# Stick-breaking scores from stacked rounded halves, stacked softmax queries, another opening order, spectra stored by another queue

## The chip, the cores and the metric
The kernel runs as one program on one core of one Trainium2 chip. The metric is the device time of one execution in microseconds (us). The kernel before takes 2325.8 us (median of three runs, 2324.95 to 2327.99). Its engines are called PE (TensorE, the matrix engine), DVE (VectorE), ACT (ScalarE), POOL (GpSimd) and SP (SyncE, which here only issues transfers).

## The reference, cut to what matters
Two blocks of two layers each, batch 1, 512 tokens, width 1024. The four places that the change touches:

```
# opening: S5 mixer
h = rms_norm(x, norm_mix[0]);  u = h @ w_in                    # (512, 1024)
ab, bb, c  ->  y = scan(u) ...                                  # complex recurrence over 64 groups

# stick-breaking attention, 16 heads of 64
z = einsum('bhqd,bhkd->bhqk', q * 64**-0.5, k)                  # float32, causal blocks only
log_one_minus = where(causal, log_sigmoid(z) - z, 0)
rem = reverse_cumsum(log_one_minus) - log_one_minus
w = where(causal, exp(log_sigmoid(z) + rem), 0);  o = w @ v

# softmax attention, first 8 of 16 heads: 8 query heads, 2 key heads, 512 queries x 768 keys
q_a, k_a = rope(rms_norm(q_a)), rope(rms_norm(k_a))             # rope on the 512 latent tokens only
s = q_a . k_a * 64**-0.5;  p = softmax(s);  o = p @ v_a

# hyena mixer: spectra of 4 filters of 512 channels, scaled and used later
k_f = rfft(filters);  z = irfft(rfft(z) * k_f) ...
```

## The kernel before, in words
All work is one straight program for each engine, written by hand; engines wait for each other on semaphores that only count up. Activations lie with channels in the partitions (8 tiles of 128 channels x 512 tokens). PSUM has 8 banks of 512 float32 columns; `take` reserves one and waits until its last reader has released it, `fills` and `frees` signal full and free.

Matrix products have two forms. In plain float32 one `matmul` of the program becomes two records of the trace. In the split form each operand is a rounded part (type fp32r, written by ACT) and a rest (value minus rounded part, written by DVE or POOL), and a product is three fp32r matmuls: hi x hi, hi x lo, lo x hi. The big layers use the split form (`lin_split`); the weight halves are rounded by ACT (`split_hi`) and their rests taken by POOL (`split_lo`, L1458).

*Opening.* SP issues its transfers in program order: parameters, `cols`, the four quarters of x, the constants `mats`, then the first weight panel, the B and C parameters, three more panels. PE first sums the squares of x for the norm (`norm("mix0")`, L417), then computes u = x W (L475) as eight tiles (nb, jt) of 6.9 us; the norm's scale is applied when ACT copies a tile out (L1137), which needs `R4` (DVE L1698). DVE and POOL build the tables of the recurrence beside it.

*Stick-breaking attention* (PE L679 to L725). `scores(h)` makes four causal blocks of 512, 384, 256 and 128 columns in plain float32: `KZ[:, h]` holds the 64 rows of head h and zeros in the other 64, so the full 128 rows of `Q` can be streamed. After each block a bfloat16 product of two constant matrices adds the mask (L681). ACT makes softplus of the scores (`Abs` L1233, `Exp` L1235, `Ln` in two parts L1240), DVE adds and splits it (L1913, L1915, L1917), PE adds running sums (`cumulate`, L691, L697, L710), and ACT's `weights` (L1247) takes the exponential, which also releases the banks of head h. PE's order is scores(h), cumulate(h-1), and for odd h the value products of two heads (`values`, L725). scores(h+1) uses the banks of head h-1, so it waits for `weights(h-1)`.

*Softmax attention.* After norms and rope, 64 turns n (head, query tile): `sm_scores(n)` on PE (two products of 384 keys, L840 for n < 32, L842 after), `sm_max` on DVE (L1974, L1978), `sm_exp` on ACT (L1303), six transposes (`sm_turn(n-2)`, L852), copied out half by ACT (L1086) and half by DVE (L1994), value products for two turns (`sm_values`, L874, L878), and a gate every fourth turn (DVE L2003, L2005). Before it DVE rotates four query tiles and one key tile (L1946, L1947, L1951), the eight products `qm` (L799) and others run on PE meanwhile.

*Spectra.* For each of four filter groups u: PE makes filters (L927), DVE decays and adds them (L2069, L2085), ACT and POOL sum absolute values (L1340, L1539), PE reduces them (L919) and transforms (L945), DVE combines (L2108 to L2111) into one buffer `SPO`, and POOL stores that to memory twice for each group (`spectra_out`, L1525). The hyena input layer (split form, 32 halves) follows.

Of the kernel before, what the change touches and what calls it, by code (L numbers as in the profile page):

```python
# [27 lines left out]
P = 128  # L28
# [42 lines left out]
def build(nc, A, out):  # L71
    ctx = ExitStack()
    with ctx:
# [38 lines left out]
        def col(n, i=0, r=P):  # L112
# [12 lines left out]
            "conv_base", "silu_ready", "kz_zero", "ln_ready", "sp_raw", "cum_done", "s_lat",  # L125
            "rn_ready",
            "w3_in",
# [50 lines left out]
        slots_used = [SLOTS]  # L178
# [127 lines left out]
        KZ = bigv(0, 8192).rearrange("p (h t) -> p h t", h=HEADS)  # L306
        VT = bigv(8192, 4096).rearrange("p (s n) -> p s n", s=4)
        Q = bigv(12288, 4096).rearrange("p (k t) -> p k t", k=KT)
# [14 lines left out]
        KZ2 = bigv(4096, 2 * LA).rearrange("p (h t) -> p h t", h=2)  # L323
        PR = [bigv(5632 + LA * i, LA) for i in range(3)]
# [79 lines left out]
        def _(pe):  # L404
# [57 lines left out]
            pe.wait_ge(S["consts_in"], 16)  # L462
            norm("mix0")

            for nb in range(4):
                s, wp = panel(pe, A["ssm_w_in"][nb][:, :], KT)
                for jt in range(2):
                    key = ("u", nb, jt)
                    o = take(pe, key, bank=(2 + 2 * nb + jt) % 4)
                    for jj in range(2):  # L470
                        for k in range(KT):
                            if nb == 0 and jt == 0 and jj == 0:
                                h_wait(k)
                            t0 = (2 * jt + jj) * P
                            i = pe.matmul(o[:, jj * 256:jj * 256 + 256], H[:, k, t0:t0 + P], wp[:, k, :],  # L475
                                          start=k == 0, stop=k == KT - 1)
                    fills(i, key)
                    if nb == 0 and jt == 0:
                        o = take(pe, ("rb", "mix0"), bank=1)
# [190 lines left out]
            def scores(h):  # L670
                key = ("z", h)
                o = take(pe, key, bank=3 * (h % 2), n=3)
                if h == 0:
                    pe.wait_ge(S["masks_ready"], 2)
                    for t in range(8):
                        pe.wait_ge(*free(("k", t)))
                        pe.wait_ge(*free(("q", t)))
# [107 lines left out]
            panel_done(s, full(key))  # L785
            lin("gate", A["in_gate"], 4, lat, beside=lambda m: norm(SMALL_NORMS[4 + m]) if m < 5 else None)
# [37 lines left out]
            def sm_scores(n):  # L824
# [3 lines left out]
                if n == 0:  # L828
                    pe.wait_ge(S["roped"], 7)
                if n == 32:  # L830
                    pe.wait_ge(S["roped"], 15)
# [118 lines left out]
            enter_halves([full(("f", 1, 1, 3))])  # L950
            lin_split(lambda t: (f"z{t // 8}" if t < 24 else "zg", t % 8), A["hy_in"], 32, h_hi_wait("nw1"), h_lo_wait("nw1"),
# [68 lines left out]
        def _(sp):  # L1020
# [4 lines left out]
            for i in range(4):  # L1025
                put(X[:, 2 * i:2 * i + 2, :], A["x"][:, 2 * i:2 * i + 2, :], f"x_in{i}")
            put(mats[:, :], A["mats"][:, :], "consts_in")
            for n, (src, dst, landed, after) in enumerate(loads):
                if n == 1:
                    put(BRAW[:, :, :, :], A["ssm_b"][:, :, :, :], "bc_in")  # L1030
                    put(CC[:, :, :, :], A["ssm_c"][:, :, :, :], "bc_in")
                for w in after:
# [9 lines left out]
        def _(act):  # L1042
# [75 lines left out]
            act.wait_ge(S["cols_in"], 16)  # L1118
            act.activation(small[:, 616:632], cols[:, COLS["c"]:COLS["c"] + 16], ACT.Silu).then_inc(S["s_lat"], 1)
            act.preload_act_table_set("sqrt_and_others")  # L1120
            for k in range(4, KT):
# [5 lines left out]
                  ("norm", "mix0"))  # L1127

# [83 lines left out]
            for t in range(8):  # L1212
# [3 lines left out]
                act.wait_ge(S["kz_zero"], t // 2 + 1)  # L1216
                act.wait_ge(*full(key))
                step(act.activation(KZ[0:64, 2 * t, :], ps(key)[0:64, :], ACT.Copy))
                own()
                frees(act.activation(KZ[64:128, 2 * t + 1, :], ps(key)[64:128, :], ACT.Copy), key)  # L1220
            for q in range(8):
                split_hi(HALVES_AT["v"] + q + 2)
            for t in range(8):
                split_hi(HALVES_AT["q"] + t + 2)
                evac(("q", t), Q[:, t, :], scale=HD ** -0.5)

            def softplus(h):
# [176 lines left out]
        def _(pool):  # L1404
# [76 lines left out]
            for m in range(8):  # L1481
                pool.wait_ge(*full(("down0", m)))
            for i in range(4):
                pool.memset(KZ[:, 4 * i:4 * i + 4, :], 0.0).then_inc(S["kz_zero"], 1)
                split_lo(HALVES_AT["k"] + 2 + i)
            for n in range(HALVES_AT["k"] + 6, HALVES_AT["ffn1"]):
# [13 lines left out]
            for t in range(8):  # L1500
                pool.wait_ge(*full(("gate", t)))
            pool.memset(bigv(4096, 2 * LA), 0.0).then_inc(S["kz_zero"], 1)
# [6 lines left out]
            pool.wait_ge(S["roped"], 15)  # L1509
# [10 lines left out]

            def spectra_out(u):
                for f in range(2):
                    n = 2 * u + f
                    pool.wait_ge(S["spec_used"], n + 1)
                    pool.dma_start(spec[u // 2, u % 2, f], SPO[:, :]).then_inc(S["spec_out"], 16)  # L1525

            for u in range(4):
# [15 lines left out]
                if u:  # L1543
                    spectra_out(u - 1)
            spectra_out(3)
# [11 lines left out]
        def _(dve):  # L1557
# [102 lines left out]
            dve.wait_ge(*free(("norm", "mix0")))  # L1660
            dve.reciprocal(rows_of("mix0"), rows_of("mix0")).then_inc(S["rn_ready"], 1)

# [34 lines left out]
            dve.wait_ge(*full(("rb", "mix0")))  # L1697
            frees(dve.tensor_copy(R4, ps(("rb", "mix0"))[:, 0:P:32]), ("rb", "mix0"))  # L1698
# [7 lines left out]
            own()  # L1706
            step(TS(BB[:, 1, :, :], BB[:, 1, :, :], -1.0, None, ALU.mult))
# [189 lines left out]
            norm_split("mix1", lambda k: col("mix1", k), r=rms[:, 0:L])  # L1897
            for c in range(2):
                for t in range(4):
                    key = ("v", c, t)  # L1900
                    dve.wait_ge(*full(key))
                    frees(dve.tensor_copy(VT[:, t, c * 512:c * 512 + 512], ps(key)), key)
            dve.tensor_copy(NEGTRI, mat("negtri")).then_inc(S["neg_ready"], 1)
# [36 lines left out]
            dve.wait_ge(S["kz_zero"], 5)  # L1940
            for t in range(5):
# [8 lines left out]
                if t < 4:  # L1950
                    TT(q, q, rt, ALU.add).then_inc(S["roped"], 1)  # L1951
                else:
                    for hh in range(2):
                        rr = slice(64 * hh, 64 * hh + 64)
                        TT(KZ2[rr, hh, LC:LA], q[rr, :], rt[rr, :], ALU.add).then_inc(S["roped"], 1)
                        step(dve.tensor_copy(KZ2[rr, hh, 0:LC], KA2[rr, 0:LC]))
            own()
            dve.sem_inc(S["roped"], 1)
# [424 lines left out]
```

## Time and profile before
| | us |
|---|---|
| runs | 2324.95, 2325.8, 2327.99; median 2325.8 |
| profiled execution | 2322.11, of it 2320.3 in the span of the engines |
| PE busy | 2176.5 (94%) |
| DVE busy | 1263.3 (54%) |
| ACT busy | 736.0 (32%) |
| POOL busy | 685.1 (30%) |
| mean granted PE clock | 0.966 of full speed |

PE is busy for 94% of the span, and a busy share says nothing of what it is busy with: a plain float32 product and a slow clock both count as busy. Where PE sits idle, the profile names what it waited for. Times are counted from the start of the span.

### The profile page before, as it was taken

The page shows a single profiled execution, that of the slowest core. Times are in us where ns is not written, and L with a number is a line of the kernel's source. Part 1 is how long each engine was busy: PE and PEld are TensorE (multiplying, and loading weights), DVE is VectorE, ACT ScalarE, POOL GpSimd, SP SyncE. Part 2 cuts the span into 40 slices and gives each one's busy share as a digit, 9 for nine tenths or more (in the row PEclk, how much of TensorE's full clock was granted, in tenths as well). Part 3 has the DMA queues.
Part 4 walks back from the last instruction along what each step waited for, and adds up shares of the span by engine and source line. Part 5 has one row for each costly group of instructions (what it writes and reads, how often), then busy time and mean ns, then how long its engine had stood idle before and what let it go on. Part 6 is the DMA issues. An engine that isn't in the chain of part 4 may idle for free. (4 is left out here: it accounts for less than half of the span.)

```text
span 2320.3 us, 27423 instructions
## 1 busy us (share of the span) xinstructions
PE 2176.5 (94%) x10821; PEld 1581.0 (68%) x10821; DVE 1263.3 (54%) x2299; ACT 736.0 (32%) x1035; POOL 685.1 (30%) x405
## 2 busy tenths in 40 slices
PE   7959899999999988999999999999999989999988
PEld 6847688888868766688888855436774436885653
DVE  8562389984352166378872032357773574235861
ACT  3423332231242365332322131325441332332110
POOL 6513344445444300345444400010000342441000
PEclk9979899999989999999999989989999979999999
DMA  4033244434423200244433231110002113322101
GB/s 177 2 49 93 73 141 149 140 122 127 138 73 91 82 1 1 82 136 136 146 125 100 75 120 55 59 36 21 1 1 73 73 73 118 100 91 91 73 19 73
DMA packets 50576, 193.66 MB, mean 83 GB/s; under 512 B 9225, under 2 KB 9401, under 8 KB 45231
## 3 DMA queue, kind: packets, MB, share of 16 engines
q1 hardware_dynamic: 36288, 140.14, 19.3%
q0 software_dynamic: 10432, 50.59, 6.0%
q10 hardware_dynamic: 3728, 1.18, 0.3%
q8 instruction: 86, 1.41, 0.2%
q14 instruction: 42, 0.34, 0.0%
HBM read 179.04 MB, written 10.49 MB: 82 GB/s over the span
## 5 line engine op out<-in xcount | busy, mean ns | idle before, releaser
L1458 POOL TENSOR_TENSOR w_lo<-raw,w_hi 128x1024 fp32r<-128x1024 f32 (+1 forms) x216 | 513.5, 2378 | 834.3 <-ACT w_hi L1096 834.1
L583 PE MATMUL psum<-h_hi,w_hi 128*128 128x512 f32 x1216 | 485.8, 400 | 10.1 <-ACT h_hi L1103 8.5
L584 PE MATMUL psum<-h_hi,w_lo 128*128 128x512 f32 x1216 | 478.2, 393 | 0.0
L1096 ACT ACTIVATE w_hi<-raw 128x1024 fp32r<-128x1024 f32 (+1 forms) x216 | 224.9, 1042 | 611.1 <-PE psum L588 400.6
L588 PE MATMUL psum<-h_lo,w_hi 128*128 128x512 f32 x1216 | 302.1, 391 | 0.0
L583 PEld LDWEIGHTS psum<-h_hi,w_hi 128*128 128x128 f32 x1216 | 230.4, 189 | 72.8 <-ACT h_hi L1103 15.9
L584 PEld LDWEIGHTS psum<-h_hi,w_lo 128*128 128x128 f32 x1216 | 231.1, 190 | 45.8 <-issue 0.2
L588 PEld LDWEIGHTS psum<-h_lo,w_hi 128*128 128x128 f32 x1216 | 229.4, 189 | 47.9
L452 PE MATMUL psum<-big,ring 128*128 128x512 f32 x480 | 208.7, 593 | 0.0
L452 PEld LDWEIGHTS psum<-big,ring 128*128 128x128 f32 x480 | 90.7, 190 | 113.7 <-issue 112.9
L630 PE MATMUL psum<-f_hi,w_hi 128*128 128x512 f32 x352 | 137.6, 391 | 0.0
L631 PE MATMUL psum<-f_hi,w_lo 128*128 128x512 f32 x352 | 137.1, 389 | 0.0
L632 PE MATMUL psum<-f_lo,w_hi 128*128 128x512 f32 x352 | 137.0, 389 | 0.0
L1086 ACT ACTIVATE big<-psum 128x384 f32<-128x384 f32 (+5 forms) x142 | 72.8, 538 | 178.9 <-PE psum L852 79.7
L1766 DVE TENSOR_TENSOR X<-psum,X 128x512 f32<-128x512 f32 x24 | 16.6, 691 | 184.6 <-PE psum L632 147.1
L1786 DVE SCALAR_TENSOR_TENSOR sq<-sq,small 128x128 f32<-128x128 f32 x210 | 104.0, 544 | 2.5
L1786 DVE SCALAR_TENSOR_TENSOR sq<-ffn_buf,small,sq 128x128 f32<-128x128 f32 x210 | 101.8, 534 | 2.5
L1198 ACT ACTIVATE ffn_buf<-psum,cols 128x512 f32<-128x512 f32 x44 | 34.4, 781 | 197.3 <-PE psum L588 197.3
L630 PEld LDWEIGHTS psum<-f_hi,w_hi 128*128 128x128 f32 x352 | 66.1, 188 | 14.3
L632 PEld LDWEIGHTS psum<-f_lo,w_hi 128*128 128x128 f32 x352 | 66.1, 188 | 13.8
L631 PEld LDWEIGHTS psum<-f_hi,w_lo 128*128 128x128 f32 x352 | 66.1, 188 | 13.2
L1576 DVE RECIPROCAL rms<-rms 128x512 f32<-128x512 f32 (+1 forms) x9 | 27.0, 2997 | 83.0 <-ACT rms L1075 83.0
(365 smaller groups left out, 3327.2 us busy)
## 6 DMA issues: line engine op xcount, KB each, us to landing
raw<-in_ffn_w_up SPq DMA_DIRECT2D x88, 512.0 KB, 3.7
raw<-in_ffn_w_down SPq DMA_DIRECT2D x32, 512.0 KB, 3.6
raw<-in_hy_in SPq DMA_DIRECT2D x32, 512.0 KB, 3.5
ffn_buf<-in_ada_w POOLq DMA_DIRECT2D x20, 512.0 KB, 5.0
sq<-in_ada_w POOLq DMA_DIRECT2D x20, 512.0 KB, 5.0
raw<-in_ssm_w_glu SPq DMA_DIRECT2D x16, 512.0 KB, 3.6
spec<-big POOLq DMA_DIRECT2D x8, 1024.0 KB, 4.1
big<-spec POOLq DMA_DIRECT2D x8, 1024.0 KB, 5.1
```

The costliest lines, as they stand in the source:

```text
L452: i = pe.matmul(o[:, 0:n], wp[:, k, m * P:(m + 1) * P], src(k), start=k == 0, stop=k == kts - 1)
L583: pe.matmul(o, hi[:, k, :], h_of(k), start=k == 0, stop=False)
L584: pe.matmul(o, lo[:, k, :], h_of(k), start=False, stop=False)
L588: i = pe.matmul(o, hi[:, k, :], l_of(k), start=False, stop=k == KT - 1)
L630: pe.matmul(o, hi[:, k, :], FHI[:, kk, :], start=kk == 0, stop=False)
L631: pe.matmul(o, lo[:, k, :], FHI[:, kk, :], start=False, stop=False)
L632: i = pe.matmul(o, hi[:, k, :], FLO[:, kk, :], start=False, stop=kk == FT - 1)
L1086: frees(act.activation(dst, ps(key) if src is None else src, func, **kw), key)
L1096: act.activation(w_hi[:, (n % 2) * HALF:(n % 2) * HALF + w], raw[:, (n % 4) * HALF:(n % 4) * HALF + w], ACT.Copy).then_inc(S["w_hi"], 1)
L1198: act.activation(CONVG[:, m % 2, :], ps((f"up{l}", 2 * m)), ACT.Identity, bias=col(f"conv{l}", 3 * FT + m), scale=col(f"conv{l}", 2 * FT + ...
L1458: pool.tensor_tensor(w_lo[:, at:at + w], raw[:, (n % 4) * HALF:(n % 4) * HALF + w], w_hi[:, at:at + w].bitcast(F32), ALU.subtract).then_in ...
L1786: i = STT(acc, ada_weights(j)[:, k, :], sv, acc, ALU.mult, ALU.add)
```

## The change
It has four parts.

1. Stick-breaking scores. `KS[:, h]` (fp32r) now holds k's rounded part in the 64 rows of head h and k's rest in the other 64; `Q_TWICE[h]` holds q's rounded part in both; `Q_LOW` holds q's rest. A block is one fp32r product over 128 rows and one over the 64 rows of `half(h)`, instead of one plain float32 product. ACT writes the rounded parts, DVE the rests (`K_REST`, `Q_LOW`), and POOL copies 64 rows to the other 64 by transfers inside SBUF (`other_half`). The zeroing of `KZ` goes. ACT's `weights(h-1)` moves from before both `Ln` parts to between them.
2. Softmax scores, n < 32. `QS[:, h]` holds q's rounded part in its own rows and its rest in the other 64; `KH` and `KL` hold k's rounded part and rest in both row halves. A product of 384 keys is two fp32r products over 128 rows. DVE makes the parts behind each rope tile, POOL copies between the row halves. `QS` lies in two of the four slots of the weight ring, so from the gate layer on only two are used; two of the three `PR` buffers move.
3. Opening. PE's u tile (0,0) comes before the norm's sums. SP issues half of x, the first panel, the other half of x, B, C, and then `mats`. DVE's reciprocal and `R4` come later, and ACT's `Silu` too.
4. Spectra. The eight stores go from POOL to SP, ahead of SP's fifth load of the hyena layer.

```diff
-        KZ = bigv(0, 8192).rearrange("p (h t) -> p h t", h=HEADS)
+        KS = f_hi[:, 0:8192].rearrange("p (h t) -> p h t", h=HEADS)
+        Q_TWICE = [(HHI, HLO)[h % 2][:, h // 2, :] for h in range(HEADS)]
+        def half(h):
+            return slice(64 * (h % 2), 64 * (h % 2) + 64)
...
+                    pe.wait_ge(S["ks_both"], 256)
+                    pe.wait_ge(S["qs_both"], 256)
                 for i in (0, 1, 3, 2):
-                    m = pe.matmul(zblk(o, i), KZ[:, h, i * P:(i + 1) * P], Q[:, h // 2, i * P:L],
-                                  start=i != 3, stop=False, skip_group_check=True)
+                    pe.matmul(zblk(o, i), KS[:, h, i * P:(i + 1) * P], Q_TWICE[h][:, i * P:L], start=i != 3, stop=False,
+                              skip_group_check=True)
+                    m = pe.matmul(zblk(o, i), KS[half(h), h, i * P:(i + 1) * P], Q_LOW[half(h), h // 2, i * P:L],
+                                  start=False, stop=False, skip_group_check=True)
...
-                if h >= 1:
-                    weights(h - 1)
                 own()
-                for lo, hi in SP_PARTS:
+                for q, (lo, hi) in enumerate(SP_PARTS):
+                    if q and h >= 1:
+                        weights(h - 1)
                     act.activation(LN_[b][:, lo:hi], LN_[b][:, lo:hi], ACT.Ln, bias=1.0).then_inc(S["ln_ready"], 1)
...
+            def other_half(sig, h, dst, src):
+                pool.dma_start(dst[half(h + 1), :], src[half(h), :]).then_inc(S[sig], 16)
...
+                    for h in (2 * t - 2, 2 * t - 1):
+                        pool.wait_ge(S["qs_hi"], h + 1)
+                        other_half("qs_both", h, Q_TWICE[h], Q_TWICE[h])
...
-                        i = pe.matmul(o[:, c, 0:384], QA[:, h // 2, qs], KZ2[:, h % 2, ks], start=True, stop=True)
+                        pe.matmul(o[:, c, 0:384], QS[:, h, qs], KH[:, h % 2, ks], start=True, stop=False)
+                        i = pe.matmul(o[:, c, 0:384], QS[:, h, qs], KL[:, h % 2, ks], start=False, stop=True)
...
+                for a in range(2):
+                    rr = slice(64 * a, 64 * a + 64)
+                    v, hi, lo, sig = (QA[rr, t, :], QS[rr, 2 * t + a, :], Q_REST[rr, t, :], "q_split") if t < 4 else \
+                        (KA2[rr, :], KH[rr, a, :], KL[rr, a, :], "k_split")
+                    dve.tensor_copy(hi, v).then_inc(S[sig], 1)
+                    dve.wait_ge(S[sig], 2 * a + 1 + (4 * t if t < 4 else 0))
+                    TT(lo, v, hi.bitcast(F32), ALU.subtract).then_inc(S[sig], 1)
...
+                if n == spectra_at[0]:
+                    for u in range(8):
+                        sp.wait_ge(S["spec_used"], u + 1)
+                        put(spec[u // 4, (u // 2) % 2, u % 2], SPO[:, :], "spec_out")
```

On PE, the scores of one head before are these rows (L679 the plain float32 blocks from `KZ`, which the trace calls big; L681 the masks):

```order
L679 MATMUL psum<-big 128x512
L681 MATMUL psum<-masks 128x128
L679 MATMUL psum<-big 128x384
L681 MATMUL psum<-masks 128x128
L679 MATMUL psum<-big 128x128
L681 MATMUL psum<-masks 128x128
L679 MATMUL psum<-big 128x256
L681 MATMUL psum<-masks 128x128
```

and these now (L690 over 128 rows, L692 over the 64 rows of the head, L694 the masks):

```order
L690 MATMUL psum<-h_hi,f_hi 128x512
L692 MATMUL psum<-f_lo,f_hi 128x512
L694 MATMUL psum<-masks 128x128
L690 MATMUL psum<-h_hi,f_hi 128x384
L692 MATMUL psum<-f_lo,f_hi 128x384
L694 MATMUL psum<-masks 128x128
L690 MATMUL psum<-h_hi,f_hi 128x128
L692 MATMUL psum<-f_lo,f_hi 128x128
L694 MATMUL psum<-masks 128x128
L690 MATMUL psum<-h_hi,f_hi 128x256
L692 MATMUL psum<-f_lo,f_hi 128x256
L694 MATMUL psum<-masks 128x128
```

Each plain product has become a pair, the second of which uses half of the array's rows.

On SP the first transfers of the program before are these:

```order
L1022 DMA small<-in_ssm_a 128x96
L1022 DMA cols<-in_cols 128x432
L1022 DMA X<-in_x 128x1024 x4
L1022 DMA mats<-in_mats 128x1024
L1034 DMA ring<-in_ssm_w_in 128x2048
L1022 DMA big<-in_ssm_b 128x1024
L1022 DMA scr<-in_ssm_c 128x1024
L1034 DMA ring<-in_ssm_w_in 128x2048 x3
```

and these now:

```order
L1041 DMA small<-in_ssm_a 128x96
L1041 DMA cols<-in_cols 128x432
L1041 DMA X<-in_x 128x1024 x2
L1059 DMA ring<-in_ssm_w_in 128x2048
L1041 DMA X<-in_x 128x1024 x2
L1041 DMA big<-in_ssm_b 128x1024
L1041 DMA scr<-in_ssm_c 128x1024
L1041 DMA mats<-in_mats 128x1024
L1059 DMA ring<-in_ssm_w_in 128x2048 x3
```

The first weight panel has moved ahead of half of x and of `mats`, and `mats` behind B and C.

On POOL the spectra stage before reads (L1536, L1539 sums of absolute values; L1525 stores; L1458 weight rests of the hyena layer):

```order
L1539 TENSOR_TENSOR sq<-sq,scr 128x512 x7
L1525 DMA spec<-big 128x2048 x2
L1458 TENSOR_TENSOR w_lo<-raw,w_hi 128x1024 x2
L1536 COPY sq<-scr 128x512
L1539 TENSOR_TENSOR sq<-sq,scr 128x512 x7
L1525 DMA spec<-big 128x2048 x4
L1458 TENSOR_TENSOR w_lo<-raw,w_hi 128x1024 x30
```

and now (L1577, L1580 the sums, L1484 the rests):

```order
L1580 TENSOR_TENSOR sq<-sq,scr 128x512 x7
L1484 TENSOR_TENSOR w_lo<-raw,w_hi 128x1024 x2
L1577 COPY sq<-scr 128x512
L1580 TENSOR_TENSOR sq<-sq,scr 128x512 x7
L1484 TENSOR_TENSOR w_lo<-raw,w_hi 128x1024 x30
```

No store stands any more between the sums and the two weight rests.

## Rows read from the trace of the kernel before

**Rows 1.** Timeline, softmax loop: start us, us, engine, line, count [idle before].
```profile
1606.24 0.56 DVE L1994 COPY big<-psum 128x384 f32<-128x384 f32 x1 [1.36 <-PE psum L852]
...
1607.46 0.96 DVE L1974 TENSOR_REDUCE small<-psum 128x1 f32<-128x768 f32 x1 [0.28 <-PE psum L840]
...
1608.54 0.56 DVE L1994 COPY big<-psum 128x384 f32<-128x384 f32 x1
...
1609.30 1.53 PE L874 MATMUL psum<-big 128*64 128x128 f32 x24
...
1611.96 0.56 DVE L1994 COPY big<-psum 128x384 f32<-128x384 f32 x1 [1.41 <-PE psum L852]
...
1615.38 1.53 PE L874 MATMUL psum<-big 128*64 128x128 f32 x24 [0.28 <-DVE big L1994]
```

**Rows 2.** The chain that ended last, its first piece: start us, us, what.
```profile
1896.68 3.01 DVE big L2085 x5
```

**Rows 3.** Timeline, PE: one head's scores begin, and the running sums behind them.
```profile
846.26 1.12 PE L679 MATMUL psum<-big 128*128 128x512 f32 x2 [1.33 <-ACT big L1247]
...
848.89 0.42 PE L691 MATMUL psum<-f_lo,tail 128*128 128x384 f32 x1
```

**Rows 4.** Timeline, PE: end of a `cumulate`, `values`, next `scores`.
```profile
851.46 0.52 PE L697 MATMUL psum<-f_lo,tail 128*128 128x384 f32 x3
851.81 0.44 PE L710 MATMUL psum<-f_lo,tail 128*128 128x512 f32 x1
852.18 2.37 PE L725 MATMUL psum<-big 128*64 128x512 f32 x16
854.49 0.70 PE L679 MATMUL psum<-big 128*128 128x512 f32 x1
```

**Rows 5.** Timeline, PE: a product on 64 rows, then full ones.
```profile
1793.33 1.07 PE L904 MATMUL psum<-sq,small 64*64 64x512 f32 x2
1794.33 4.99 PE L452 MATMUL psum<-big,ring 128*128 128x512 f32 x11
```

**Rows 6.** Timeline, PE: first scores, first running sum.
```profile
794.61 1.10 PE L679 MATMUL psum<-big 128*128 128x512 f32 x2 [1.78 <-ACT big L1086]
...
802.58 0.41 PE L691 MATMUL psum<-f_lo,tail 128*128 128x384 f32 x1 [2.58 <-DVE f_lo L1915]
```

**Rows 7.** Small POOL transfers of L1431 (x2) and L1510 (x1), issue to landing.
```profile
DMA to landing us min/median/max: 2.3/2.6/3.0
DMA to landing us min/median/max: 4.0/4.0/4.0
```

**Rows 8.** A stretch: PE, PEld, DVE, ACT, POOL busy, then granted PE clock, DMA share, GB/s.
```profile
803.00:806.00 3.00, 3.00 (x16) 2.74 (x16) 2.15 (x4) 0.80 (x1) 0.00 (x0) 0.67 0.03 5
```

**Rows 9.** DVE by line: a rounding copy (ns min/median/max; first and last start; forms).
```profile
L1915 DVE CAST f_lo<-scr x16: 426/493/560, 801.9 to 911.0; 128x768 fp32r<-128x768 f32 x8, 128x512 fp32r<-128x512 f32 x8
```

**Rows 10.** Timeline, PE: five rotated tiles (first four here), then the `qm` tiles.
```profile
1516.73 3.60 PE L792 MATMUL psum<-Hb,mats 128*128 128x512 f32 x8
...
1521.02 9.18 PE L799 MATMUL psum<-big,ring 128*96 128x512 f32 x21
```

**Rows 11.** Timeline, opening: PE and ACT.
```profile
11.42 1.93 PE L417 MATMUL psum<-big,mats 128*32 128x128 f32 x32 [11.42 <-DMA mats<-in_mats]
...
18.56 9.04 PE L475 MATMUL psum<-ring,Hb 128*128 128x256 f32 x32
...
76.10 0.98 ACT L1137 ACTIVATE big<-psum,small 128x256 f32<-128x256 f32 x2 [5.93 <-PE psum L475]
```

**Rows 12.** Transfers of the first 60 us in 40 slices, GB/s.
```profile
GB/s 0 143 274 369 341 388 418 442 404 412 445 431 410 426 415 120 0 0 0 0 0 0 0 60 268 363 8 0 0 0 0 0 19 254 391 44 3 0 0 0
```

**Rows 13.** Timeline: ACT, DVE and POOL in the spectra stage.
```profile
1887.21 2.00 ACT L1096 ACTIVATE w_hi<-raw 128x1024 fp32r<-128x1024 f32 x2
...
1890.49 9.20 DVE L2085 TENSOR_TENSOR big<-big 128x512 f32<-128x512 f32 x8 [0.51 <-PE psum L927]
...
1891.00 5.13 POOL L1458 TENSOR_TENSOR w_lo<-raw,w_hi 128x1024 fp32r<-128x1024 f32 x2
```

More of the change, by code:

```diff
@@ L1127, in _ @@
                   ("norm", "mix0"))
+            act.wait_ge(S["cols_in"], 16)
+            act.activation(small[:, 616:632], cols[:, COLS["c"]:COLS["c"] + 16], ACT.Silu).then_inc(S["s_lat"], 1)
             for nb in range(4):
@@ L1215, in _ @@
                 split_rows("mix1", (t,), QHI)
-                act.wait_ge(S["kz_zero"], t // 2 + 1)
                 act.wait_ge(*full(key))
-                step(act.activation(KZ[0:64, 2 * t, :], ps(key)[0:64, :], ACT.Copy))
-                own()
-                frees(act.activation(KZ[64:128, 2 * t + 1, :], ps(key)[64:128, :], ACT.Copy), key)
+                for h in (2 * t, 2 * t + 1):
+                    act.activation(KS[half(h), h, :], ps(key)[half(h), :], ACT.Copy).then_inc(S["ks_hi"], 1)
             for q in range(8):
@@ L1224, in _ @@
                 split_hi(HALVES_AT["q"] + t + 2)
-                evac(("q", t), Q[:, t, :], scale=HD ** -0.5)
+                act.wait_ge(*full(("q", t)))
+                for h in (2 * t, 2 * t + 1):
+                    act.activation(Q_TWICE[h][half(h), :], ps(("q", t))[half(h), :], ACT.Copy, scale=HD ** -0.5) \
+                        .then_inc(S["qs_hi"], 1)
             def softplus(h):
@@ L1706, in _ @@
             own()
+            dve.wait_ge(*full(("rb", "mix0")))
+            frees(dve.tensor_copy(R4, ps(("rb", "mix0"))[:, 0:P:32]), ("rb", "mix0"))
             step(TS(BB[:, 1, :, :], BB[:, 1, :, :], -1.0, None, ALU.mult))
@@ L1896, in _ @@
             dve.wait_ge(*free(("rb", "kv")))
-            norm_split("mix1", lambda k: col("mix1", k), r=rms[:, 0:L])
+            for t in range(8):
+                norm_split("mix1", lambda k: col("mix1", k), ks=(t,), r=rms[:, 0:L])
+                dve.wait_ge(*full(("k", t)))
+                for h in (2 * t, 2 * t + 1):
+                    dve.wait_ge(S["ks_hi"], h + 1)
+                    i = TT(K_REST[t][half(h), :], ps(("k", t))[half(h), :], KS[half(h), h, :].bitcast(F32), ALU.subtract)
+                    if h % 2:
+                        frees(i, ("k", t))
+                    else:
+                        step(i)
+                        own()
+            dve.wait_ge(S["ks_both"], 256)
             for c in range(2):
@@ L1902, in _ @@
                     frees(dve.tensor_copy(VT[:, t, c * 512:c * 512 + 512], ps(key)), key)
+            for t in range(8):
+                dve.wait_ge(*full(("q", t)))
+                for h in (2 * t, 2 * t + 1):
+                    dve.wait_ge(S["qs_hi"], h + 1)
+                    i = STT(Q_LOW[half(h), t, :], ps(("q", t))[half(h), :], HD ** -0.5,
+                            Q_TWICE[h][half(h), :].bitcast(F32), ALU.mult, ALU.subtract)
+                    if h % 2:
+                        frees(i, ("q", t))
+                    else:
+                        step(i)
+                        own()
             dve.tensor_copy(NEGTRI, mat("negtri")).then_inc(S["neg_ready"], 1)
@@ L1949, in _ @@
                 dve.wait_ge(*free(key))
[L1950 to L1958, printed above, removed]
+                step(TT(q, q, rt, ALU.add))
+                own()
+                for a in range(2):
+                    rr = slice(64 * a, 64 * a + 64)
[4 more added lines that the diff above has]
+                    TT(lo, v, hi.bitcast(F32), ALU.subtract).then_inc(S[sig], 1)
             def sm_rope(h):
```

92 lines of the change are left out of this document (53 added, 39 removed).

## The prediction
> **What bounds the kernel now.** I read the stretches first (busy time and clock), then the timeline at each place that the change touches, and last the chain that ended last. PE is busy for 94% of the span and works in program order; the end moves only where PE does less, works faster, or waits less. Two places are bound otherwise, and the reader should see both. In the softmax loop, every second DVE copy of transposed weights (L1994) is followed almost at once by PE's value products (L874), in one round with a recorded wait of 0.28 us [rows 1]: a circle of PE and DVE is as long as PE's own work. In the spectra stage the chain runs through DVE's additions (L2085) [rows 2].
>
> **Part 1, stick-breaking scores.** One head's scores take 848.89 - 846.26 = 2.63 us [rows 3]. The fp32r products of 384, 256 and 128 columns take 851.81 - 851.46 = 0.35 us, 0.46 ns a column [rows 4]. Two passes over 1280 columns are then 1.17 us; the four masks and the small blocks' weight loads, some 0.5 us together by what the plain scores take beyond 4 passes (2.63 - 2.13), stay. So 1.7 us if the new order of products costs nothing.
>
> It may not. Each block now goes from 128 rows to 64 and back. The one place where the trace does this is L904: its two records take 2 x 0.427 us of columns (512 columns twice at 2.4 GHz for each record), so it ends at 1794.18, and the next full product starts at 1794.33, 0.15 us later [rows 5]. From full width to 64 columns the step is 852.18 - 851.81 = 0.37 us for a product of 512 columns at 0.23: 0.14 us [rows 4]. In and out is thus up to 0.29 us, four times a head 1.2 us. The ends for the new scores are 1.7 us and 2.9 us. Part of it falls on the masks' and small blocks' gaps, which I counted once already; I take 2.4 us, a saving of 0.2 us a head. (TensorEngine Tiling (Array Packing), section Key Properties, of the Trainium skill says that changing the tiling mode drains TensorE. The trace agrees for 64 rows with 64 columns, by 0.15 us behind the product; no row shows 64 rows with all 128 columns. By the rule the scores take about 2.4 us, without it 1.7.)
>
> Fourteen heads lie behind the first running sum, so 14 x 0.2 = 2.8 us go. Against this, ACT's first `Ln` part now stands before `weights`. Where no `values` covers it, PE waits for `weights` (1.33 us [rows 3]); ACT reaches `weights` about 0.2 us later, an estimate at a ns a column: Abs, Exp (1280 columns each) and `Ln` (768) end 3.6 us behind the scores, the running sums 3.4. Seven heads: +1.2 us. The loop: **-1.6 us**.
>
> Its start is later. Today PE idles 1.78 us and begins at 794.6 [rows 6]. Now the last q tile is followed by ACT's rounding of a weight half, two half copies (ending about 795.2) and POOL's two transfers, the second issued about 795.1 to 795.3. Small POOL transfers land 2.3 to 4.0 us after issue [rows 7]; I take 2.8, near the middle of the three, so scores start at 798.0: +3.4 us (ends +2.9 and +4.6). PE has then idled 5.2 us. Behind 2.58 us of idle time the granted clock was 0.67 [rows 6, 8], that is partly 1.2 GHz, so scores(0) run slower: +1.5 us. The chain from there to the first running sum (ACT, then DVE) is as before; with scores(0) at 2.4 instead of 2.6 us this is **+4.7 us**. The other steps (K's rests on DVE, POOL's copies beside the k tiles) have the 24 fp32r products of a tile (0.23 us each) and eight banks to hide in; cover gone, each subtraction would cost its 0.6 us. The dropped zeroing of `KZ` holds up nothing today.
>
> **Part 2, softmax.** DVE gets four more operations per rope tile: two copies (0.43 [rows 9]) and two subtractions (0.6, as L2085 [rows 2]), with their waits about 2.1 us, so a tile takes 4.2 us instead of 2.0. Tile t's bank is released at its first operation. The first rotated tile is full at 1517.6, so tile 4 is released at 1517.8 + 4 x 4.2 + 0.7 = 1535.2. The banks turn by eight: qm tile 7 takes the bank of rotated tile 4, and PE reaches it at 1521.02 + 7 x 1.72 = 1533.1 [rows 10]. **+2.1 us** (ends 0 and +4). DVE is then free by 1540, well before PE's next need of it, behind the qm tiles and sixteen smaller ones. The ring's two slots are refilled in some 4 us (1 MB at the rate of part 3), while a panel serves 16 plain products of 0.85 us.
>
> In the loop PE's scores shrink. Plain products take 2.31 / 1280 = 1.8 ns a column (854.49 - 852.18, two heads side by side [rows 4]), fp32r 0.46: 2 x 384 x 1.8 = 1.39 us become 4 x 384 x 0.46 = 0.70, so 0.69 a turn. But the circle with DVE holds no scores: copy to maximum 1606.24 to 1607.46 less the wait of 0.28, 0.94; maximum to copy 1.08; copy to value products 0.76 at most, of which I take 0.70; value products and transposes to the next copy 2.66 [rows 1]. Sum 5.38 us for two turns without a gate, against 5.72 now; with a gate on DVE (about 0.8) 6.1 or more, which is what it is now (1615.38 - 1609.30 = 6.08, with the wait). Eight rounds x 0.34: **-2.5 us**. The ends are 0 and 16 x 1.38 = -22.
>
> **Part 3, opening.** `mats` lands at 11.4 [rows 11], and half of x and `mats` are 1.5 MB that now follow the panel. By the sizes in SP's order 2.9 MB had come by then, and the transfers run at about 410 GB/s [rows 12]; so the panel (byte 2.4 million) lands near 10.0 instead of 14, x's last quarter near 12.7, `mats` near 16.5. PE starts u near 10.1 in place of 18.56, at first at half speed and in the pace of x: 19.2 for tile (0,0) in place of 27.4. The norm's sums follow, 2.2 us (twice the 32 records of L417 in 1.93 us, at full clock about half of that), then seven tiles of 6.9, a wait of 0.5 for `R4` (about 36.0, PE is there at 35.6) and 0.3 for the transposes. That ends at 70.5 to 71, where the last tile now ends at 75.9 [rows 11]. Nothing behind it, neither DVE's tables nor POOL's (both have over 10 us to spare, and POOL starts 1.3 us later) is late. All that follows, the scan and the transfers of T, hangs on this. **-5.0 us** (ends -2 and -6).
>
> **Part 4, spectra.** POOL did its two weight rests at 1891.0 to 1896.1, behind the stores, though ACT was done at 1888.2 and 1889.2. DVE's eight additions beside them took 9.2 us [rows 13]; the last five, alone, took 3.0, 0.6 each [rows 2], so eight alone would take 4.9. Now POOL can start at 1888.3 and end near 1893.4. Half of that falls beside DVE operations that read PSUM. **-2.0 us** (ends -4 and 0). SP's queue holds the fifth hyena half behind the eight stores until about 1941; its load and rounding are needed four tiles of 5.5 us behind 1934.
>
> **Sum.** -1.6 + 4.7 + 2.1 - 2.5 - 5.0 - 2.0 = -4.3 us. On the profiled execution's 2322.1 that is 2317.8. This execution lies 3.7 us below the median shown (2325.8), so I predict 2321.5.
>
> **Rivals.**
> - *The change of rows costs nothing.* Scores of 1.7 us save 0.9 on each of 14 heads: 13 us instead of 2.8, and about 0.9 less in the start. -4.3 - 11 = -15: 2310. For it: the one row has 64 columns too [rows 5]. Against it: every change of shape in rows 4 and 5 left a gap of 0.14 us or more (851.81 to 852.18, 854.49, 1794.33).
> - *The softmax circle opens.* If DVE can take the additional slack in rounds with a gate, PE's own work of 5.72 - 1.38 = 4.3 us bounds, up to -22 instead of -2.5. I would expect half at best: -10 more, 2311. Against it: the recorded wait of L874 for DVE [rows 1].
> - *Slower by the clock.* The pause of PE in each second head of the stick-breaking loop is 1.33 us now [rows 3] and becomes about 1.5, in a round of 15 us. The clock stays full with 1.33. Should it fall at the longer pause, PE runs some 4 us at 1.2 GHz each time, +2 us in seven rounds, 14 us: -4.3 + 14 = +10, 2335. It decides once the pause is at the clock's limit. For it: the drop at 803 behind 2.58 us [rows 6, 8]. Against it: 1.78 us of idle at 794.6 was followed by full clock until 800.
> - *The copies come late.* Transfers that cast or wait take 4.0 us or more and the start costs 3 us more, with 2.9 us scores: +8, 2330.
>
> **How the numbers follow.** Forecast 57%, free rows 23%, open circle 7%, clock 5%, late copies 8%. Within the forecast the unknown terms give -10 to +2, so 2316 to 2328. The range for 8 in 10 is 2308 to 2329. About 0.2% (4.7 us) is what a measurement of this kernel can tell from no change. The forecast is at the edge of it, 2321.5 against 2321.1: half of its chance falls on faster (0.28), nearly half on the same (0.27), little on slower (0.02). With the rivals: faster 0.58, same 0.30, slower 0.12.
>
> **What would show it.** Right: the two products of a block (L690, L692) start about 0.1 us further apart than 0.46 ns a column; PE idles over 4 us before the first scores; L799's last tile waits for DVE; rounds of two softmax turns of 5.4 and 6.1 us with PE waiting for L1994's successor; the last u tile ends near 71; DVE's eight additions take about 7 us. Wrong: scores of 1.7 us, softmax rounds under 5.2 us, a clock below 0.9 within the stick-breaking loop, or PE waiting for a ring slot.

## The result and the profile after

The changed kernel takes 2354.3 us (median of 4 runs, 2352.6 to 2355.8); the kernel before took 2325.6 in the same comparison. The ratio is 1.012 (95% interval 1.0105 to 1.0135): 28.7 us slower. I predicted 2321.5 with a range of 2308 to 2329; both were wrong, and so was the sign. The profiled execution is 2354.4 us with a span of 2352.6; its span is 32.3 us longer than that of before, because the profile of before lay 3.5 us under its median.

The two traces are compared by the start of the same piece of work in each.

| place (PE) | before | after | later by |
|---|---|---|---|
| first transpose behind the u tiles | 77.33 | 73.87 | -3.5 |
| last q tile done | 792.83 | 790.80 | -2.0 |
| first running sum | 802.58 | 806.29 | +3.7 |
| last `values` of stick-breaking | 921.79 | 954.97 | +33.2 |
| first rotated tile (rope) | 1516.73 | 1550.63 | +33.9 |
| first softmax scores | 1565.14 | 1603.69 | +38.6 |
| late round of softmax | 1750.91 | 1785.40 | +34.5 |
| last wait for the filter additions | 1920.83 | 1953.67 | +32.8 |
| last normalisation | 2309.79 | 2342.07 | +32.3 |

One stage makes the result: from the first running sum to the last `values`, 119.2 us became 148.7. PE's timeline there, one head at full clock, its running sum, the pause, and the next head (start us, us, engine, line, idle before):

```profile
875.58 0.49 PE L690 MATMUL psum<-h_hi,f_hi 128*128 128x512 f32 x1
876.01 0.50 PE L692 MATMUL psum<-f_lo,f_hi 64*128 64x512 f32 x1
876.44 0.23 PE L694 MATMUL psum<-masks 128*128 128x128 bf16 x1
876.48 0.42 PE L690 MATMUL psum<-h_hi,f_hi 128*128 128x384 f32 x1
...
878.42 0.42 PE L704 MATMUL psum<-f_lo,tail 128*128 128x384 f32 x1
...
883.24 0.51 PE L690 MATMUL psum<-h_lo,f_hi 128*128 128x512 f32 x1 [1.80 <-ACT big L1273]
...
887.38 0.67 PE L704 MATMUL psum<-f_lo,tail 128*128 128x384 f32 x1
```

Answering to [rows 3]: the scores take 878.42 - 875.58 = 2.84 us at full clock where they took 2.63, and 887.38 - 883.24 = 4.14 in the next head. PE's pause for ACT's `weights` is 1.80 us instead of 1.33. Why the second head is slow stands in the stretches (PE, PEld, DVE, ACT and POOL busy, then granted clock, DMA share, GB/s):

```profile
876.00:880.00 4.00, 4.00 (x25) 2.98 (x25) 2.53 (x5) 1.32 (x2) 0.00 (x0) 1.00 0.00 0
880.00:884.00 4.00, 2.20 (x12) 1.45 (x10) 1.76 (x3) 3.68 (x4) 0.00 (x0) 1.00 0.00 0
884.00:888.00 4.00, 4.00 (x13) 2.48 (x13) 2.43 (x4) 0.34 (x1) 0.00 (x0) 0.50 0.00 0
888.00:892.00 4.00, 4.00 (x22) 3.70 (x22) 0.00 (x0) 3.01 (x3) 0.00 (x0) 0.65 0.00 0
892.00:896.00 4.00, 4.00 (x23) 1.90 (x23) 3.84 (x6) 1.76 (x2) 0.00 (x0) 1.00 0.01 2
```

Behind each pause of 1.80 us the granted clock is at its lower level (1.2 GHz) for some 7 to 10 us, though PE is busy the whole time. The first 30 us of the stage, behind the idle time of 5.45 us, lie at 0.5 nearly throughout. The whole stage, before and then after:

```profile
794.00:922.00 128.00, 110.41 (x626) 77.03 (x628) 76.15 (x110) 81.78 (x82) 2.34 (x1) 0.99 0.02 5
```

```profile
796.00:955.00 159.00, 143.34 (x626) 100.39 (x627) 76.76 (x112) 81.08 (x80) 0.36 (x1) 0.74 0.01 4
```

0.99 became 0.74, with nearly the same DVE and ACT time. The other stages went nearly as forecast. Rope, to [rows 10]:

```profile
1554.93 10.46 PE L813 MATMUL psum<-big,ring 128*96 128x512 f32 x24
1565.73 1.96 PE L813 MATMUL psum<-big,ring 128*96 128x512 f32 x4 [0.34 <-DVE scr L2004]
1570.12 3.60 PE L813 MATMUL psum<-big,ring 128*96 128x512 f32 x4 [2.44 <-DVE scr L2004]
1573.65 10.53 PE L821 MATMUL psum<-big,ring 128*64 128x256 f32 x32
```

PE waits 2.78 us for banks of rotated tiles, and the four products behind the wait take 3.60 us where the four ahead took 1.96. The softmax loop, to [rows 1], a round without and one with a gate:

```profile
1628.44 1.53 PE L892 MATMUL psum<-big 128*64 128x128 f32 x24 [1.37 <-DVE big L2052]
...
1633.73 1.53 PE L892 MATMUL psum<-big 128*64 128x128 f32 x24 [0.57 <-DVE big L2052]
...
1639.81 1.53 PE L892 MATMUL psum<-big 128*64 128x128 f32 x24 [1.35 <-DVE big L2052]
```

The rounds are 5.29 and 6.08 us (forecast 5.38 and 6.1), and PE now waits for DVE in every one. The opening, to [rows 11], and DVE's additions, to [rows 13]:

```profile
11.64 9.80 PE L481 MATMUL psum<-ring,Hb 128*128 128x256 f32 x32 [11.64 <-DMA ring<-in_ssm_w_in]
21.37 1.95 PE L426 MATMUL psum<-big,mats 128*32 128x128 f32 x64
...
73.87 1.33 PE L503 MATMUL psum<-mats,big 128*64 128x64 f32 x38 [1.27 <-ACT big L1162]
```

```profile
1925.64 7.12 DVE L2143 TENSOR_TENSOR big<-big 128x512 f32<-128x512 f32 x8 [0.51 <-DVE big L2169]
```

### The profile page after: what moved, and what is told of

Same layout as the page of the kernel before. It is cut to its first block and busy times, and to the rows that moved or that the text cites. A ratio compares the mean times of both kernels' runs of the same rounds, so it can differ in the third digit from the quotient of the medians.

```text
span 2352.6 us, 27538 instructions
## 1 busy us (share of the span) xinstructions
PE 2199.7 (94%) x10821; PEld 1609.0 (68%) x10821; DVE 1294.3 (55%) x2348; ACT 741.8 (32%) x1043; POOL 695.1 (30%) x436
## 3 DMA queue, kind: packets, MB, share of 16 engines
q1 hardware_dynamic: 37440, 148.53, 20.1%
## 5 line engine op out<-in xcount | busy, mean ns | idle before, releaser
L1484 POOL TENSOR_TENSOR w_lo<-raw,w_hi 128x1024 fp32r<-128x1024 f32 (+1 forms) x216 | 513.4, 2377 | 896.8 <-ACT w_hi L1121 896.6
L1111 ACT ACTIVATE big<-psum 128x384 f32<-128x384 f32 (+6 forms) x134 | 68.2, 536 | 175.1 <-PE psum L870 71.1
L640 PEld LDWEIGHTS psum<-f_hi,w_lo 128*128 128x128 f32 x352 | 66.1, 188 | 13.2
```

The costliest lines, as they stand in the source:

```text
L640: pe.matmul(o, lo[:, k, :], FHI[:, kk, :], start=False, stop=False)
L1111: frees(act.activation(dst, ps(key) if src is None else src, func, **kw), key)
L1484: pool.tensor_tensor(w_lo[:, at:at + w], raw[:, (n % 4) * HALF:(n % 4) * HALF + w], w_hi[:, at:at + w].bitcast(F32), ALU.subtract).then_in ...
```

## The experiments

Each comparison has its own runs of the kernel before (medians 2325.6 to 2327.3). "Loop" is, in each profile, the time from the first running sum to the last `values`; "clock" the mean granted clock from the first scores to the last `values`.

| kernel | 2nd product | weights | us | ratio (95%) | loop | clock |
|---|---|---|---|---|---|---|
| before | (plain) | early | 2325.6 | | 119.2 | 0.99 |
| after | 64 rows | late | 2354.3 | 1.0105 to 1.0135 | 148.7 | 0.74 |
| e1_order | 64 rows | early | 2344.7 | 1.0067 to 1.0097 | 134.9 | 0.83 |
| e2_rows | 128 rows | late | 2313.8 | 0.9931 to 0.9960 | 109.3 | 0.93 |
| e3_both | 128 rows | early | 2322.7 | 0.9976 to 0.9995 | 117.3 | 0.93 |
| e4_no_stick | (plain) | early | 2320.1 | 0.9965 to 0.9983 | 119.3 | 0.99 |
| e5_grouped | 64, grouped | late | 2335.9 | 1.0023 to 1.0053 | 135.1 | 0.75 |
| e6_few_cols | 64, 128 columns | late | 2345.6 | 1.0066 to 1.0096 | 143.6 | 0.74 |
| e7_before_late | (plain) | late | 2337.0 | 1.0026 to 1.0059 | 128.4 | 0.91 |
| e8_start | 128 rows | late | 2312.8 | 0.9923 to 0.9953 | 110.9 | 0.91 |
| e9_fill | 64 rows | late | 2338.1 | 1.0024 to 1.0052 | 128.8 | 0.89 |
| e10_late_fill | (plain) | late | 2328.1 | 0.9991 to 1.0010 | 118.3 | 0.99 |
| e11_best | 128 rows | late | 2299.7 | 0.9862 to 0.9900 | 110.8 | 0.92 |
| e12_best_fill | 128 rows | late | 2308.2 | 0.9895 to 0.9925 | 106.2 | 0.96 |

**e1_order, e2_rows, e3_both, e4_no_stick.** The order (shown as the change from after; `weights` goes back to its old place) and the rows:

```
-                own()
-                for q, (lo, hi) in enumerate(SP_PARTS):
-                    if q and h >= 1:
-                        weights(h - 1)
+                if h >= 1:
+                    weights(h - 1)
+                own()
+                for q, (lo, hi) in enumerate(SP_PARTS):
```

```
-   m = pe.matmul(zblk(o, i), KS[half(h), h, i * P:(i + 1) * P], Q_LOW[half(h), h // 2, i * P:L],
+   m = pe.matmul(zblk(o, i), KS[:, h, i * P:(i + 1) * P], Q_LOW[:, h // 2, i * P:L],
```

With all 128 rows in the second product, the other 64 rows add this head's key rest times the neighbouring head's query rest, which the reference does not have. e3 is both edits; e4 is the kernel before with all parts of the diff except those of stick-breaking.

> The changed kernel with one thing put back: ACT does the weights of the head before ahead of both Ln parts of a head, as in the kernel before. Theory A (the clock falls because PE's pause in each second head grew from 1.33 to 1.80 us): the pause returns to about 1.35 us, the granted clock between 840 and the end of the stick-breaking loop is 1.00 in every 4 us, and the loop is 20 to 25 us shorter, so about 2332. Theory B (the clock falls because of the 64-row products and the changes of rows around them, not because of the pause): the pause returns too, but the clock still shows stretches of 0.5 in each round, and the time falls only by 7 x 0.47 = 3 us, to about 2351. Theory C (the clock is low because the 5.45 us of idle time ahead of the first scores put PE in a state it does not leave): as B, with the low clock from the start on.

> The changed kernel with its second product of a block on all 128 rows instead of the head's own 64, so no product of the scores changes rows. [...] Theory A (pause): the pause stays near 1.8 us, so the clock still falls to 0.5 once a round; a head's scores take 1.8 us where the clock is full instead of 2.84, 14 x 1.0 = 14 us less, 2340. Theory B (rows): the clock is full behind the first 40 us though the pause is 1.8 us, and with the shorter scores the loop ends some 35 to 40 us earlier: 2315 to 2320. The price of the row changes itself is read in both cases as 2.84 less the scores here.

> Both edits together: weights ahead of both Ln parts, and the second product on all 128 rows. Theory A: pause about 1.35 us, clock 1.00, scores 1.8 us: 2332 - 14 = 2318. Theory B: the same as with full rows alone, less 3 us at most: 2313 to 2317. If scores at 1.8 us make ACT the later one, the pause is longer by what PE saves (0.8 us a head) and neither saves more than half of its sum.

> The kernel before with the opening, softmax and spectra parts of the change, and without the stick-breaking part. By the offsets of the two profiles: the opening -3.5 us at its end, of which -1.4 to -3 still stand at the second half of the stage behind it, rope and softmax together +4.6 - 4.1 = +0.5, spectra -1.6: about 2322 (range 2319 to 2324). If instead these parts cost by what they move elsewhere (queues, clock), it is 2326 or more, and the stick-breaking part costs less than the 31.5 us by which its loop grew.

Neither theory as I had put it holds. With 64 rows and a pause of 1.33 us (e1) the clock still falls, but not in each round: the six rounds from 823 on take 18.2, 15.4, 18.3, 15.4, 18.3 and 18.2 us. One of its pauses, and the stretch behind it:

```profile
890.46 0.50 PE L690 MATMUL psum<-h_lo,f_hi 128*128 128x512 f32 x1 [1.33 <-ACT big L1273]
...
892.00:896.00 4.00, 4.00 (x19) 3.44 (x19) 3.44 (x6) 2.20 (x2) 0.00 (x0) 0.61 0.00 0
```

With full rows and a pause of 1.80 us (e2) it falls behind the pauses at 817.49 and 832.65, whose rounds take 15.2 us, and from 837 on it stays full, in rounds of 13.6 us with the same pause. Two stretches of e2, behind the pause that ends at 832.65 and behind the one that ends at 847.81:

```profile
832.00:836.00 4.00, 3.35 (x13) 2.43 (x14) 3.77 (x6) 1.11 (x2) 0.00 (x0) 0.60 0.00 0
848.00:852.00 4.00, 4.00 (x30) 3.50 (x30) 2.97 (x5) 2.48 (x3) 0.00 (x0) 1.00 0.00 0
```

So the length of a pause does not decide alone. Theory C does not hold either: e2 has the same idle time ahead of its first scores (5.54 us) and leaves the low clock. The scores of e2:

```profile
847.81 0.50 PE L690 MATMUL psum<-h_lo,f_hi 128*128 128x512 f32 x1 [1.82 <-ACT big L1273]
848.15 0.39 PE L692 MATMUL psum<-f_lo,f_hi 128*128 128x512 f32 x1
...
849.55 0.42 PE L704 MATMUL psum<-f_lo,tail 128*128 128x384 f32 x1
```

1.74 us, so the eight changes of rows of a head cost 2.84 - 1.74 = 1.10 us, 0.14 us each. The late weights cost 9.6 us with 64 rows (after less e1) and save 8.9 us with 128 rows (e2 against e3). A round takes 13.60 us in e2 and 14.63 in e3, though e3's pause is the shorter one (1.33 us). The saving is in waits of e3 that e2 does not have; there PE is ready before DVE has split the softplus:

```profile
848.77 0.44 PE L704 MATMUL psum<-f_lo,tail 128*128 128x384 f32 x1 [0.45 <-DVE f_lo L1974]
```

With the first `Ln` part ahead of `weights`, DVE starts earlier. (Smaller delays of the same kind follow: four products of L710 take 0.95 us in e3 and 0.63 in e2.) e4 shows that opening, softmax and spectra together gain 6.2 us (2326.3 to 2320.1) and that the stick-breaking part costs 34 (2354.3 - 2320.1).

**e5_grouped, e6_few_cols, e7_before_late, e8_start.** In e5 the four 64-row products of a head stand behind its other products; in e6 each is cut to the first 128 columns of its block; e7 is the order alone, on the kernel before. In e8, made from e2:

```
-                    pe.wait_ge(S["qs_both"], 256)
+                    pe.wait_ge(S["qs_both"], 224)
+                if h == 14:
+                    pe.wait_ge(S["qs_last"], 32)
...
-                        other_half("qs_both", h, Q_TWICE[h], Q_TWICE[h])
+                        other_half("qs_last" if t == 8 else "qs_both", h, Q_TWICE[h], Q_TWICE[h])
```

> The changed kernel with the four 64-row products of a head one behind the other, behind the four full-row products and their masks, so PE goes to 64 rows and back once a head instead of four times. The columns done on 64 rows are the same 1280. Theory B1 (what drops the clock is the time PE loses at each change of rows): six of eight changes go, 6 x 0.14 = 0.8 us a head, scores at full clock 2.84 - 0.8 = 2.0 us, the clock is full behind the first 30 us, and the time is 2354 - 31 = about 2323 or below. Theory B2 (what drops it is the columns that run on half of the rows): scores as short, but the clock falls to 0.5 once a round as before, 2340 to 2345.

> The changed kernel with its 64-row product of each block cut to the block's first 128 columns (the low part of the query is left out for the other columns): the four changes to 64 rows and back stay, 768 of 1280 columns at 64 rows go. Scores at full clock 2.84 - 768 x 0.46 ns = 2.49 us. Theory B1 (changes): the clock still falls to 0.5 once a round, 2345 to 2352. Theory B2 (columns on half of the rows): the clock is full behind the first 30 us, 2354 - 31 = 2323 or a little below.

> The kernel before with one thing of the change: the weights of the head before stand between the two Ln parts instead of ahead of both. No 64-row product. Theory A (pause): the pause in each second head becomes about 1.8 us and the clock falls to 0.5 in parts of each round, 2326 + 15 or more. Theory B: the pause grows, the clock stays full, and a round changes by what the order does alone: the rounds with full rows were 13.60 us with the late weights and 14.63 us with the early ones, so 15.20 us become about 14.3, seven rounds, 2326 - 6 = 2320. By my prediction's step for it (+1.2 us in all) it would be 2327.

> The version with all products on 128 rows and late weights, and the first scores no longer behind the two half copies of the last query tile: heads 0 to 13 wait for the first 14 copies, head 14 for the last two. PE's idle time of 5.5 us ahead of the first scores goes or falls below 2 us, so the clock stays full at the start; ACT, whose first Abs began at 799.9, is free at 794.6 (the end of its table load at 794.5), so the first running sum is at most 5.3 us earlier: 2313.8 - 5 = 2309, and up to 5 us more if the clock, which showed 0.5 to 0.9 in the stretches from 796 to 836, stays at 1.00. If the idle time only moves behind the first scores (as the 2.6 us of the kernel before), the gain is 3 us or less.

e5: the scores take 2.06 us at full clock, (2.84 - 2.06) / 6 = 0.13 us for each change that went, and the time falls by 18 us, yet the clock's mean is 0.75 as before, with a pause of 1.67 us. e6: the same 0.74. So taking away most of the changes of rows alone, or most of the 64-row columns alone, does not keep the clock up; without both (e2) it is full from 837 on. e7 is what I had called the clock rival, by itself: pause 1.82 us, and in each round a stretch like the middle one here:

```profile
850.80 1.13 PE L679 MATMUL psum<-big 128*128 128x512 f32 x2 [1.82 <-ACT big L1247]
...
848.00:852.00 4.00, 2.18 (x10) 1.25 (x10) 2.21 (x3) 3.24 (x4) 0.00 (x0) 1.00 0.00 0
852.00:856.00 4.00, 4.00 (x16) 2.79 (x16) 1.99 (x4) 0.88 (x1) 0.00 (x0) 0.58 0.00 0
856.00:860.00 4.00, 4.00 (x27) 2.66 (x28) 1.32 (x2) 3.94 (x5) 0.00 (x0) 1.00 0.02 4
```

Rounds of 16.98 instead of 15.20 us, the loop 9.2 us longer, 2337.0 against 2327.3. No key, query or product differs from before: only the order of ACT's work, and with it half a microsecond of pause. e8 took 2312.8, which cannot be told from e2's 2313.8 (2309 was expected): the scores start behind 3.87 instead of 5.5 us of idle time, not at once, because PE now waits for the copies of the tile before, which land some 5 us after their issue. POOL's half copies, in the changed kernel, from issue to landing (min, median, max):

```profile
DMA to landing us min/median/max: 2.2/5.0/5.6
```

The last two landed in 2.2 and 2.4 us (PE starts 2.8 us behind the issue of the second); those beside the load of a weight half for most of their time took about 5. That the load is the reason is not shown.

**e9_fill, e10_late_fill, e11_best, e12_best_fill.** The fillers, in e9 (six) and, with plain products of 384 columns, in e10 (two), ahead of the scores of each odd head from 3 on; the bank is that of the next `values`, which overwrites it:

```
+                if 3 <= h < HEADS and h % 2:
+                    fill((h - 3) // 2, 6)
...
+   pe.matmul(o, KS[:, 0, 0:P], KS[:, 1, :], start=True, stop=True, skip_group_check=True)
```

> The changed kernel (64-row products, late weights) with six more fp32r products of 512 columns, 1.4 us of work whose result is overwritten, in PE's pause of 1.80 us in each second head of the loop from head 3 on. Nothing else is shorter or longer. If the clock falls by what PE leaves idle in a round, the pause and the row changes together, the filled pause brings the clock back to 1.00 in most or all of each round and the loop is up to 7 x 3.5 = 25 us shorter: 2330 to 2340. If the 64-row products alone drop it, the time stays at 2354, or is some us longer.

> The kernel before with late weights (which alone took 2337.0, with a pause of 1.82 us and the clock at 0.5 for some 3 us of each round of 17.0 us), and two plain products of 384 columns, 1.4 us of work, in that pause. If the idle time drops the clock, it is 1.00 in the whole loop, a round takes 15.3 us again, and the time is 2325 to 2328. If the order of ACT's work costs by itself, the rounds stay near 17 us.

> The version with all products on 128 rows and late weights, with three more edits: the scores of heads 0 to 7 wait only for the copies of the first four query tiles (head 8 and head 14 for the later ones), ACT loads its table ahead of the last query tile's rounding, and in the rope stage DVE rotates all five tiles before it splits any. The start: PE goes on at once behind the last query tile (4 us of idle time go from here, and stand behind the scores of heads 0 and 1 instead), the first Abs begins near 793.3 instead of 797.9: 4 us. Rope: PE's waits of 2.4 and 0.3 us for L2004 go: 2.8 us, if the copies of the halves behind it are not late (they have 30 us). 2312.8 - 6.8 = 2306. If the idle time only moves at the start: 2310.

> The same version with 16 more fp32r products of 512 columns (3.7 us of work whose result is overwritten) behind the scores of head 1, where PE waits for the first running sum. If the idle time there is what takes the clock to 0.5 to 0.8 in the 20 us behind it, the clock is 1.00 and the loop begins 5 to 8 us faster: about 2299. If the drop comes from elsewhere, it is the same as without them.

e9 is the changed kernel plus work, and is 16 us faster. PE's timeline in it, in a later round:

```profile
881.91 0.50 PE L690 MATMUL psum<-h_hi,f_hi 128*128 128x512 f32 x1
...
887.62 1.55 PE L736 MATMUL psum<-f_hi 128*128 128x512 f32 x6
889.59 0.49 PE L690 MATMUL psum<-h_lo,f_hi 128*128 128x512 f32 x1 [0.42 <-ACT big L1287]
...
897.67 0.50 PE L690 MATMUL psum<-h_hi,f_hi 128*128 128x512 f32 x1
```

The round is 15.76 us instead of 18.6 to 20.1, and from 868 on every stretch of 4 us shows 1.00, with all 64-row products in place. The two rounds from 837.68 and 854.98 have filled pauses too and still take 17.3 and 18.8 us, with the clock low in parts. e10 does the same for e7: clock 0.99, loop 118.3, the time of the kernel before.

```profile
846.58 1.45 PE L723 MATMUL psum<-big 128*128 128x384 f32 x4
848.56 1.13 PE L679 MATMUL psum<-big 128*128 128x512 f32 x2 [0.53 <-ACT big L1261]
```

Its rounds take 15.31 us, so of the 1.8 us by which e7's rounds grew the order of ACT's work is worth 0.1, and the clock the rest. So idle time in the loop is what lowers the clock with plain products (e7, e10) and most of what lowers it with 64-row products (e9); that these add to it is seen in e1, where the pause of the kernel before is no longer harmless.

e11_best joins e8 with a finer gate, an earlier table load, and rope rotated for all tiles before any is split (`for t in range(5):` ahead of the splits). It takes 2299.7 us, ratio 0.9881 (0.9862 to 0.9900): 27 us faster than before, and the best here. The rope stage no longer waits for banks: from the first rotated tile to the first softmax scores it takes 48.2 us, and 53.1 in e8. At the start of stick-breaking PE goes on at once, but idles behind head 0's scores instead:

```profile
798.42 0.77 PE L694 MATMUL psum<-h_lo,f_hi 128*128 128x512 f32 x1 [3.02 <-issue]
```

The profile names no releaser. DVE's last subtraction from the last query tile ends 0.1 us earlier, which agrees with head 1 waiting for that tile's bank. The four executions of e11 took 2298.3 to 2307.2 us, and its rows are from the longest of them. Against e8's profiled execution (2314.3) they show 7 us, of which rope is 5; where the rest of the 13 us between the medians comes from stays open.

e12's fillers raise the stage's clock from 0.92 to 0.96, but the first running sum is later by nearly as much as the loop is shorter (13.2 us from the first scores instead of 9.0; loop 106.2 instead of 110.8). Its median of 2308.2 is above e11's, where 2299 was expected: no gain. Why it is 8.5 us above e11's these rows do not show, as they compare e11's longest execution with e12's shortest (2304.7).

## Why the prediction was wrong

- **Opening, -5.0:** measured -3.5 at the u tiles' end. The panel landed at 11.6, not 10.0 (9.97 to 12.2 in the profiles of the variants). The order of the work was right. By the end of the q tiles 2.0 is left.
- **Stick start, +4.7:** the idle time grew from 1.78 to 5.45 (I had 5.2), and from first scores to first running sum 7.97 became 10.04 us: +5.7 in all. Right in kind, the clock's share too small. The 2.8 us for POOL's copies had no row of their own kind behind it: the transfers of [rows 7], the one of 4.0 us too, are loads from memory and not copies inside SBUF. That the value came out right is in part luck.
- **Stick loop, -1.6: this step failed.** Measured +29.5, mainly because the clock, which the sum left at full speed in this loop, had a mean of 0.74 from the first scores on. The step held three things. Scores: "I take 2.4 us" of 1.7 to 2.9; it was 2.84, since the changes cost 0.14 us each in full, eight a head, as [rows 4, 5] had shown, and my reason for discounting them (gaps counted already) was wrong. `weights`: "about 0.2 us later" was 0.47. And the clock, to which I gave 5%: the rival said +2 us a round if the pause decides it. e7 shows just that, +1.8 us a round. Against the rival I had set that "1.78 us of idle at 794.6 was followed by full clock until 800". That is a single pause; the loop's comes every 15 us, and with 64-row products PE has further small gaps in the scores. Both grew in the changed kernel. That the repetition makes the difference is my reading; no run tests it. Alone, the late weights cost 9.2 us of loop (e7), and the stacked products with their changes of rows and the longer idle time ahead of the stage 15.7 (e1 against before); together they cost 29.5.
- **Rope, +2.1:** the waits are 2.78 us, and with the half-speed products behind them and in the stage +4.7 (33.9 to 38.6). Right place, and again the clock behind a wait was left out.
- **Softmax loop, -2.5:** -4.1; rounds 5.29 and 6.08 as worked out to 0.1 us. The circle of PE and DVE bounds, as said.
- **Spectra, -2.0:** -1.6; DVE's eight additions 7.12 us against about 7 forecast.
- **Rivals:** "the change of rows costs nothing" is refuted by 1.10 us a head. Most of its 13 us were there to be had: e2 removes the changes, and its loop is 9.9 us shorter than before. Late copies: the last two landed as soon as I had taken, the earlier ones took some 5 us with no one waiting.

The Trainium skill's page TensorEngine Tiling (Array Packing), section Key Properties, says that changing the mode drains TensorE; the runs agree, for 64 rows with 128 columns too, by 0.14 us a change. The page TensorE: Matmul & The Clock Gate, section "HAM oscillation — how this bites in real kernels", warns of idle gaps that take the clock down, but of gaps longer than any in this loop. The measurement decides: gaps of 1.8 us, one in each round, did it with plain products (e7), and gaps of 1.3 us beside 64-row products (e1), while gaps of 1.3 us with plain products did not.

What stays open: how a 64-row product counts against a pause. e5 and e6 each left one half of the cause and found the same low clock, so no run prices them singly. Nor does a run show why the clock falls behind some pauses of e1, e2 and e9 and not behind others of the same length.

## What to carry to other kernels

Where PE's clock is full at a pause that repeats, it may be near falling: price a longer pause at half speed for the several microseconds behind it, in every round (3 to 10 us here). Small gaps inside PE's work probably count with it; their share was not measured. Before shortening a product to half of the rows, do it on all rows if what the other rows add is zero or negligible; the saved rows save no time (a head's scores take 1.74 us on all rows in e2, and 2.06 us with two changes of rows in e5), and each change costs 0.14 us. And a wait on ACT's or DVE's order is worth moving in one version of a loop and harmful in another: test it beside the change it comes with.

## What I had not expected of the hardware

- Adding 1.4 us of useless products per round made the kernel 16 us faster (e9), and took all of e7's loss away (e10).
- 0.49 us more of pause in a round of 15 us cost 1.8 us of it (e7), while the same pause of 1.80 us, in e2, cost some clock in two early rounds and none in the rounds of 13.6 us behind them.
- The granted clock fell in some rounds of e1 and not in others: the same code took 15.4 us in two rounds and 18.2 to 18.3 in the other four.
